# Modulation rows in four buffers, weights of the feed-forward tiles split two tiles ahead, and two mixer units in other banks, in a three-block float32 network on one core

## What is computed

```python
for layer in range(2):                          # blocks 1 and 2
    shift, scale, gate = split(c @ mod_w[layer, 0] + mod_b[layer, 0], 3)
    h = rms_norm(x, ...) * (1 + scale) + shift
    x = x + gate * rms_norm(mixer(h), ...)
    shift, scale, gate = split(c @ mod_w[layer, 1] + mod_b[layer, 1], 3)
    h = rms_norm(x, ...) * (1 + scale) + shift
    x = x + gate * rms_norm((silu(g) * u) @ w_out, ...)   # g, u = split(h @ w_in), width 2816
# block 3: modulation from silu(c_2) @ w_ada, its own mixer, then
z = conv3(h @ w_up) + b_conv;  a, b = split(z);  x = x + gt2 * ((silu(a) * b) @ w_down)
out = rms_norm(x, g_final)
```

## Time and profile before

| | us |
|---|---|
| three runs | 1174.82 median, 1167.96 to 1181.9 |
| the profiled execution | 1180.2 |
| its span in the profile | 1178.4 |
| TensorE matmul busy in the span | 1056.1 (90%) |
| VectorE busy | 791.8 (67%) |
| ScalarE busy | 552.5 (47%) |
| read from HBM | 225 MB, 192 GB/s over the span |

### The profile page before, as it was taken

The page is one execution under the profiler, slowest core; times in us unless marked ns, Lnnn a source line. Parts: engine busy times, 40 slices in busy tenths (PEclk is TensorE's granted clock), DMA queues, the critical chain, the costliest instruction groups (busy, mean ns, idle before and its releaser), DMA issues.

```text
span 1178.4 us, 21390 instructions
## 1 busy us (share of the span) xinstructions
PE 1056.1 (90%) x8164; PEld 1002.2 (85%) x8164; DVE 791.8 (67%) x1288; ACT 552.5 (47%) x1116; POOL 4.6 (0%) x14
## 2 busy tenths in 40 slices
PE   6988989988889979899988988988879879999996
PEld 5987778988889979799988887988857879999996
DVE  4649865766677656774766776765674757777775
ACT  2446755433333354454533333445441356666663
POOL 0100000000000000000000000000000000000000
PEclk9999989999999999999998999999875989999998
DMA  9966672667666637405376767664530354455530
GB/s 367 319 222 220 236 251 76 246 249 267 241 242 265 236 123 236 158 1 197 110 248 228 256 233 262 255 230 152 168 125 1 104 201 155 166 169 173 174 127 36
DMA packets 62405, 227.54 MB, mean 193 GB/s; under 512 B 7010, under 2 KB 7266, under 8 KB 61956
## 3 DMA queue, kind: packets, MB, share of 16 engines
q1 hardware_dynamic: 61556, 224.02, 53.6%
q0 software_dynamic: 640, 2.10, 0.7%
q10 hardware_dynamic: 144, 0.52, 0.1%
HBM read 225.04 MB, written 1.57 MB: 192 GB/s over the span
## 4 chain that ended last, share of the span: by engine, by line
PE 27%; DVE 24%; DMA 21%; issue 12%; ACT 12%; SPq 3%; DVEq 1%; ACTq 0%
DMA modbuf<-in_mod_w 12%; DMA modbuf<-in_w_ada 8%; DVE wL L1182 7%; ACT wH L766 5%; PE bank L1821 5%; PE bank L1822 4%; PE bank L1823 4%; DVE acc L589 2%; PE bank L1835 2%; PE bank L1836 2%; DVE proj L1383 2%; SPq L610 1%; DVE acc L1383 1%; PE bank L2428 1%; ACT pr L905 1%
## 5 line engine op out<-in xcount | busy, mean ns | idle before, releaser
L1821 PE MATMUL bank<-hH,wH 128*128 128x258 f32 (+1 forms) x1544 | 447.4, 290 | 15.0 <-DVE hL L1247 7.7
L1822 PE MATMUL bank<-hL,wH 128*128 128x258 f32 (+1 forms) x1544 | 440.0, 285 | 0.0
L1823 PE MATMUL bank<-hH,wL 128*128 128x258 f32 (+1 forms) x1544 | 438.1, 284 | 0.0
L1182 DVE TENSOR_TENSOR wL<-raw,wH 128x1024 fp32r<-128x1024 f32 x270 | 321.6, 1221 | 80.8 <-ACT wH L766 80.6
L1821 PEld LDWEIGHTS bank<-hH,wH 128*128 128x128 f32 x1544 | 294.7, 191 | 23.8 <-issue 14.8
L1822 PEld LDWEIGHTS bank<-hL,wH 128*128 128x128 f32 x1544 | 295.5, 191 | 0.5
L1823 PEld LDWEIGHTS bank<-hH,wL 128*128 128x128 f32 x1544 | 295.7, 191 | 0.0
L766 ACT ACTIVATE wH<-raw 128x1024 fp32r<-128x1024 f32 x270 | 271.1, 1045 | 35.9 <-DMA raw<-in_weights 18.6
L1821 PE MATMUL bank<-aH,wH 128*128 128x256 f32 x592 | 179.7, 304 | 58.9 <-DVE aL L1439 53.5
L1821 PEld LDWEIGHTS bank<-aH,wH 128*128 128x128 f32 x592 | 119.5, 202 | 69.6 <-DVE aL L1439 46.2
L1822 PE MATMUL bank<-aL,wH 128*128 128x256 f32 x592 | 173.7, 293 | 0.0
(11 more groups left out here) (313 smaller groups left out, 1188.3 us busy)
## 6 DMA issues: line engine op xcount, KB each, us to landing
raw<-in_weights SPq DMA_DIRECT2D x270, 512.0 KB, 4.5
modbuf<-in_mod_w SPq DMA_DIRECT2D x83, 512.0 KB, 5.0
modbuf<-in_w_ada SPq DMA_DIRECT2D x48, 512.0 KB, 5.0
strips<-bias_table POOLq DMA_DIRECT2D x8, 256.0 KB, 6.4
otok<-in_cmp_w SPq DMA_DIRECT2D x4, 512.0 KB, 8.6
raw<-in_mod_w SPq DMA_DIRECT2D x2, 512.0 KB, 4.8
otok<-in_mod_w SPq DMA_DIRECT2D x2, 512.0 KB, 10.5
sn<-in_mod_w SPq DMA_DIRECT2D x2, 512.0 KB, 11.9
```

The lines of the kernel that those rows point to most:

```text
L1182: V.tensor_tensor(wL[:, slot, :], raw[:, slot, :], wH[:, slot, :].bitcast(F32), ALU.subtract).then_inc(lo_ready[c], 1)
L1821: mm(out, lhs_h, rhs_h, start=start, stop=False, skip_group_check=True)
L1822: mm(out, lhs_h, rhs_l, start=False, stop=False, skip_group_check=True)
L1823: return mm(out, lhs_l, rhs_h, start=False, stop=stop, skip_group_check=True)
```

## The change

There are four row buffers for the jobs from f0 on (three in `modbuf`, one in `strips[:, 4:6]`), each with its own semaphore, and the load of job d waits until job d - 4 is done. In f0 and f1 the splits of a step are those of gate and up of tile t + 2 and of down(t+1): high and low of gate stand after silu and L1406, those of up after `aH` and `aL`, then comes the second job, then down. In f2 the low split of down(t) stands after the scaling and those of gate and up of tile t + 2 after the convolution and after L1436. In cd and sb units 2 and 3 go to banks 0 and 1, and only units from 4 on wait for a scaled one.

```diff
@@ -258,6 +258,7 @@
         lo_ready = [sem(f"lo_ready{i}") for i in range(3)]
         unit_used = [sem(f"unit_used{i}") for i in range(3)]
         mod_full = [sem(f"mod_full{i}") for i in range(2)]
+        job_full = [sem(f"job_full{i}") for i in range(4)]
         start_full = [sem(f"start_full{i}") for i in range(16)]
         mod_used = sem("mod_used")
         kc_zero = sem("kc_zero")
@@ -463,6 +464,8 @@
 
             if phase == "ab":
                 return bank[4 + AB_NUMBER[e] % 2]
+            if e in (2, 3):
+                return bank[e - 2]
             last = NPROJ[phase] - e
             return bank[4 + e % 2] if last > 2 else bank[4 - last]
 
@@ -527,6 +530,7 @@
             return a[:, at + j * P:at + (j + 1) * P]
 
         strips_flat = strips[:, :, :, :].rearrange("p a s j -> p (a s j)")
+        spare_job = strips[:, 4:6, :, :].rearrange("p a s j -> p (a s j)")
         third = [acc1[:, n * D:(n + 1) * D] for n in range(3)]
         start_slots = [raw[:, 4, :], raw[:, 5, :], otok[:, 0, :], sn[:, :, :].rearrange("p a b -> p (a b)"),
                        pr[:, :, :].rearrange("p a b -> p (a b)"), otok[:, 1, :], modbuf[:, 0, :], modbuf[:, 1, :],
@@ -537,14 +541,19 @@
 
         def job_value(d):
 
-            return 16 * ((d - JOBS_END["start"]) // 2 + 1)
+            if d < JOBS_END["ab"]:
+                return 16 * ((d - JOBS_END["start"]) // 2 + 1)
+            return 16 * ((d - JOBS_END["ab"]) // 4 + 1)
 
         def job_buffer(d):
 
             if d < JOBS_END["start"]:
                 q = ON_VECTOR[d]
                 return start_slots[q], start_full[q], 16
-            return modbuf[:, d % 2, :], mod_full[d % 2], job_value(d)
+            if d < JOBS_END["ab"]:
+                return modbuf[:, d % 2, :], mod_full[d % 2], job_value(d)
+            n = (d - JOBS_END["ab"]) % 4
+            return (modbuf[:, n, :] if n < 3 else spare_job), job_full[n], job_value(d)
         mod_src = [A["mod_w"][m] for m in range(4)] + [A["w_ada"][:, 0:MW], A["w_ada"][:, MW:2 * MW]]
 
         def cls(p):
@@ -612,7 +621,9 @@
             def load_job(d):
 
                 m, k, col, _, _ = JOBS[d]
-                if d >= JOBS_END["start"] + 2:
+                if d >= JOBS_END["ab"] + 4:
+                    sp.wait_ge(mod_used, d - 3)
+                elif JOBS_END["start"] + 2 <= d < JOBS_END["ab"] + 2:
                     sp.wait_ge(mod_used, d - 1)
                 dst, landed, _ = job_buffer(d)
                 sp.dma_start(dst, mod_src[m][k * P:(k + 1) * P, col:col + D]).then_inc(landed, 16)
@@ -694,9 +705,9 @@
                         for n in range(2):
 
                             d = d0 + 2 * t + n
-                            sp.wait_ge(mod_used, i * 4 + (d - 1))
+                            sp.wait_ge(mod_used, i * 4 + (d - 3))
                             src = mod_src[m + 1 + t % 2][bass.ds(i * P + P, P), n * D:(n + 1) * D]
-                            sp.dma_start(modbuf[:, d % 2, :], src).then_inc(mod_full[d % 2], 16)
+                            sp.dma_start(job_buffer(d)[0], src).then_inc(job_buffer(d)[1], 16)
 
                 assert Cursor.job == d0
                 step(0)
@@ -877,11 +888,7 @@
                     def at(n, per):
                         return n if i is None else i * per + n
 
-                    b = base + 3 * (t + 1)
-                    split = 1 <= t < FT - 1 or (t == FT - 1 and phase != "f2")
-                    if split:
-                        split_high(b, i)
-                        split_high(b + 1, i)
+                    nxt = base + 3 * t + 5
                     up_class, up_count = cls(base + 3 * t + 1)
                     act.wait_ge(unit_used[up_class], at(up_count, 2))
                     for n, bk in enumerate(gu_banks(phase, t)):
@@ -892,6 +899,7 @@
                         act.wait_ge(g_scaled, at(g0 + t + 1, 2))
                         nc.scalar.activation(sn[:, t % 2, 0:S], sn[:, t % 2, 0:S], ACT.Silu,
                                              bias=fcol[:, t % 2, 0:1]).then_inc(silu_ready, 1)
+                        split_high(nxt + 1, i)
                     else:
 
                         row = conv[:, t] if i is None else conv[:, bass.ds(i * 2 + t, 1)].rearrange("p o c -> p (o c)")
@@ -906,8 +914,9 @@
                                                         ACT.Identity, bias=row[:, 4 * n + 3:4 * n + 4],
                                                         scale=row[:, 4 * n + 1:4 * n + 2])
                         last.then_inc(zc_ready, 1)
-                        if split:
-                            split_high(b + 2, i)
+                        if nxt + 2 < N_UNITS:
+                            split_high(nxt + 1, i)
+                            split_high(nxt + 2, i)
                         act.wait_ge(conv_ready, at(t + 1, 2))
                         nc.scalar.activation(sn[:, t % 2, 0:S], pr[:, t % 2, 0:S], ACT.Silu).then_inc(silu_ready, 1)
                     act.wait_ge(af_ready, at(g0 + t + 1, 2))
@@ -916,11 +925,10 @@
                         down_class, down_count = cls(base + 3 * (t - 2) + 2)
                         act.wait_ge(unit_used[down_class], at(down_count, 2))
                     nc.scalar.activation(aH[:, t % 2, :], sn[:, t % 2, S:2 * S], ACT.Copy).then_inc(aH_ready, 1)
-                    if split and phase != "f2":
-                        if t == FT - 1:
-                            split_high(b + 3)
-                            split_high(b + 4)
-                        split_high(b + 2, i)
+                    if phase != "f2":
+                        split_high(nxt + 2, i)
+                    if 1 <= t and nxt < N_UNITS:
+                        split_high(nxt, i)
 
                 assert hi.at == base + RING
                 step(0)
@@ -1378,21 +1386,16 @@
                         cc = cvec[:, 0] if m + 1 + t % 2 < 4 else csil[:, :]
                         acc, at0 = JOBS[d][3:]
                         half = acc[:, at0:at0 + D]
-                        dve.wait_ge(mod_full[d % 2], i * 32 + job_value(d))
+                        dve.wait_ge(job_buffer(d)[1], i * 16 + job_value(d))
                         dve.wait_ge(mod_used, i * 4 + d)
-                        V.scalar_tensor_tensor(out=half, in0=modbuf[:, d % 2, :], scalar=cc[:, bass.ds(i + 1, 1)],
+                        V.scalar_tensor_tensor(out=half, in0=job_buffer(d)[0], scalar=cc[:, bass.ds(i + 1, 1)],
                                                in1=half, op0=ALU.mult, op1=ALU.add).then_inc(mod_used, 1)
 
                 def step(t, i=None):
                     def at(n, per):
                         return n if i is None else i * per + n
 
-                    b = base + 3 * (t + 1)
-                    split = 1 <= t < FT - 1 or (t == FT - 1 and phase != "f2")
-                    if split:
-                        split_low(b, i)
-                        if phase != "f2":
-                            split_low(b + 1, i)
+                    nxt = base + 3 * t + 5
                     dve.wait_ge(col_ready, at(g0 + t + 1, 2))
                     if t == 0:
                         dve.wait_ge(rstd_ready, NORMS.index(f"A{m}") + 1)
@@ -1406,12 +1409,12 @@
                         V.scalar_tensor_tensor(out=sn[:, t % 2, S:2 * S], in0=pr[:, t % 2, 0:S],
                                                scalar=fcol[:, t % 2, 1:2], in1=sn[:, t % 2, 0:S],
                                                op0=ALU.add, op1=ALU.mult).then_inc(af_ready, 1)
-                        job(1, t, i)
+                        split_low(nxt + 1, i)
                     else:
                         V.tensor_tensor(sq[:, t % 2, 0:S], gate_bank[:, 0:S], rstd[:, :], ALU.mult)
                         V.tensor_tensor(sq[:, t % 2, S:2 * S], up_bank[:, 0:S], rstd[:, :], ALU.mult).then_inc(gu_scaled, 1)
-                        if split:
-                            split_low(b + 1, i)
+                        if t >= 2:
+                            split_low(nxt - 3, i)
 
                         row = conv[:, t] if i is None else conv[:, bass.ds(i * 2 + t, 1)].rearrange("p o c -> p (o c)")
                         dve.wait_ge(zc_ready, at(t + 1, 2))
@@ -1429,20 +1432,22 @@
                                                          scalar=row[:, 4 * n + 2:4 * n + 3], in1=dst[:, 0:S - 1],
                                                          op0=ALU.mult, op1=ALU.add)
                         ins.then_inc(conv_ready, 1)
-                        if split:
-                            split_low(b + 2, i)
+                        if nxt + 2 < N_UNITS:
+                            split_low(nxt + 1, i)
                         dve.wait_ge(conv_ready, at(t + 1, 2))
                         dve.wait_ge(silu_ready, at(g0 + t + 1, 2))
                         V.tensor_tensor(sn[:, t % 2, S:2 * S], sn[:, t % 2, 0:S], pr[:, t % 2, S:2 * S],
                                         ALU.mult).then_inc(af_ready, 1)
```

(16 more changed lines are left out.)

## The result

The changed kernel takes 1235.05 us (median of 4 runs, 1232.1 to 1241.66), the kernel before 1177.68 us (4 runs). The ratio is 1.051, with a 95% interval of 1.042 to 1.059: slower by 5%, about 57 us. The profiled execution of the changed kernel took 1232.3 us with a span of 1230.5, 52 us over the span before.

The account below looks back on a forecast made before the run. Bound: in f0 and f1, a loop of low split, weight load, row DMA and VectorE's products. +74.5 (f0, f1) - 11 (f2) - 1 (mixers) = +62.5 us on the median 1174.8: 1237 us, range 1206 to 1262.

Parts of the forecast that it names:

- The loop, and that the buffers do nothing in it: f0 and f1: down's low split, SyncE's loads, row DMA, products, next low split form one loop; four buffers change nothing.
- Two splits on the path: f0 and f1: two splits of 1.14 us move behind the row, net +1.98 and +1.94 us a tile.
- The tail tiles, the start and the end: f0 and f1 outside the loop: one-row intervals +1.3 us each, 3.9 a stage; start +1.4, end +0.6.
- f2 at TensorE's pace: f2: period falls from 9.29 us to TensorE's 8.6 to 8.75; -11 us over 18 tiles, ends 0 and -14.
- The banks at about nothing: cd and sb: units 2 and 3 in banks 0 and 1; -1 us for both, ends 0 and -3.5.
- TensorE's pauses: f0 and f1: TensorE waits about 3.8 us a tile for `aL` instead of 1.8, 44 times, over 120 us in all.
- The clock rival: f0 and f1: pauses keep TensorE at 1.2 GHz, 17.3 us a tile, another +134, 1371 us; chance 0.05.
- the milder one: f0 and f1: rows land in 4.9 us, as transfers before are further apart; +31, 1206 us; chance 0.13.
- The faster one: f0 and f1: rows run ahead in four buffers, TensorE's 8.7 us a tile; 70 us shorter, 1105 us; chance 0.08.

Follow-up runs that it names:

- experiment 1: The changed kernel with two row buffers as before the change, all else kept; 1238.5 us, ratio 1.053 to the kernel before.
- experiment 4: The changed kernel with rows first: a step's row loads ahead of its three weight loads in SyncE's queue; 1110.1 us, ratio 0.944 to the kernel before.
- experiments 3 and 6: 3: changed kernel, f0/f1 splits in old places, 1166.6 us. 6: gate's split back, 1228.7; also second job, 1208.2; extra operation behind L1406, 1285.2, ahead of first product, 1236.3.
- experiment 7: The kernel before with only units 2 and 3 of cd and sb in banks 0 and 1; 1174.9 us against 1174.7, ratio 1.000.

## Why the prediction was right

It gave 1237 us, +62.5; measured are 1235 us and +57 (+50 to +70 by the interval of the ratio). The mechanism is the one that the experiments show. That the absolute times agree within 2 us is partly luck. The sum had f0 and f1 too large, +74.5 where 67 were measured in the profiled execution, and f2's gain too large as well, -11 where 7 were measured, so the two misses take from each other. And the sum started from a median before of 1174.8 us, where the one beside the result is 1177.7. The steps, one by one:

- **The loop, and that the buffers do nothing in it.** Shown. SyncE waits at the weight load before and after, experiment 1 has the loss with two buffers, and experiment 4, in which nothing but SyncE's order differs, removes the wait for the row altogether.
- **Two splits on the path, +2.28 a tile, less the second row's wait of 0.30 and 0.34.** Shown in kind by experiments 3 and 6. In size it was a little too much: +1.65 and +1.50 a tile were measured in place of +1.98 and +1.94. The term mis-sized is the time from the split of down to the first product, which I kept at 5.9 and 6.1 us. Its mean is 5.4 and 5.6 us in the changed kernel. But it did not fall by the change. In the kernel of experiment 7, with the old loop and 10.2 us a tile, it is 5.3 and 5.6 us. So I had taken it from an execution in which the rows land late: the first rows of f0's loop took 4.9 us in the median from issue to landing in the profiled execution before, and 4.2 us both in experiment 7 and in the changed kernel. Against experiment 7 a tile of the changed kernel is 1.90 and 1.84 us longer, close to what I forecast, though experiment 7 waits longer for its second rows, 0.65 and 0.49 us in the mean, than I had put. The profiled execution before lay 5.4 us over the median, and its f0 and f1 are 5.5 us longer than those of experiment 7; I took its stalls for those of every execution. In all f0 and f1 lost 67 us in the profiled execution (65.5 in the stages, 0.3 ahead and 1.2 behind) instead of 74.5, and 71 us in the stages against experiment 7.
- **The tail tiles, the start and the end.** Four of the six intervals between one-job tiles take 10.1 to 10.5 us as expected (9.26 + 1.3 = 10.6); in the other two a row lands late (12.84 us at tile 19 of f0, 11.60 us in f1). So the three of a stage cost +6.0 and +4.6 us where I had put +3.9. From the last L1406 to the next stage +0.6 us in both, as put.
- **f2 at TensorE's pace.** The period is 8.64 us in the mean of the last 19 intervals, and TensorE is busy all the time in the window shown. The gain is 7.0 us and not 11: the period of 9.29 that I took holds up to tile 16 only, the last intervals were at 8.8 us and less already, and the mean of the same 19 before was (1161.93 - 990.06)/19 = 9.05.
- **The banks at about nothing.** Measured 0, between the ends.
- **TensorE's pauses.** I had put 3.8 us a tile; the waits for `aL` are up to 4.0 us, but in all only this:

```profile
PE bank L1826 <- DVE aL L1444: 92.5, 40, 4.0
```

  The mean is 2.3 us, 92.5/40. The pause is shorter than I put since TensorE's own work takes longer: it is busy 128.74/13 = 9.9 us a tile in f0 and 10.1 in f1, where rows first has 8.65. The granted clock explains part of this. It is 0.94 and 0.90 in the two loops, where f1 had 0.96 before and rows first has 1.00. With the two levels of 2.4 and 1.2 GHz, a mean of 0.94 is 12% of 157.56 us at the lower one, of which half is lost: by this estimate 9.5 us, or 0.7 us a tile; in f1 it is 1.2. What makes up the rest of the 1.25 and 1.5 us is open. The clock rival was right about the sign of this and wrong about its weight: the loop of the rows, 12.1 us, is longer than TensorE's 9.9, so the time does not show it. One pause of f0's loop and the work behind it, in windows of PE, PEld, DVE, ACT, POOL, clock, DMA share and GB/s:

```profile
244.00:247.00 3.00, 0.42 (x4) 0.21 (x2) 2.46 (x3) 0.67 (x2) 0.00 (x0) 1.00 0.94 377
...
248.00:250.00 2.00, 2.00 (x10) 2.00 (x11) 2.00 (x2) 0.76 (x3) 0.00 (x0) 0.50 0.09 37
251.00:258.00 7.00, 7.00 (x59) 6.88 (x58) 2.49 (x5) 1.46 (x2) 0.00 (x0) 1.00 0.74 256
```

  The Trainium skill's page "TensorE: Matmul & The Clock Gate", section "HAM oscillation — how this bites in real kernels", describes a loop in which the clock falls again in every turn. Here it falls after some of the pauses only (between 220 and 280 us after two of four), and it costs nothing, for VectorE's loop sets the end.

Of the rivals, the milder one (rows that land in 4.9 us since the transfers are further apart) is not borne out: from split to first product it is 5.4 and 5.6 us, and no more than in the old loop of experiment 7. The faster one (1105 us) would have been right about the pace of f0 and f1 if the rows had run ahead: rows first gives 1110 us. Only its premise, that buffers are enough for it, was wrong.

## What to carry to other kernels

A deeper buffer is only worth something if the queue that fills it can get to the load in time: look at what stands ahead of the load in the issuing queue and what that waits for, before adding buffers. Here two buffers and a load moved up three places gave 5%, and four buffers without the move gave at most half a per cent.

In a loop that waits for a transfer, work on the waiting engine is free ahead of the wait, up to the wait's length, and costs its whole length behind it, as long as it doesn't fill another wait. Here one operation of 1.14 us in every tile cost 1.3 us in all ahead of it and 50 us behind it. So moving work off the start of a step is moving it out of its cover. Costs in such a loop don't add: taking one of two splits out gave 0.1 us, since a wait for another engine stood under it.

## What was not expected of the hardware

The time from issue to landing of the same row in the same place of the same queue differs between executions of one loop: the first rows of a tile in f0 took 4.9 us in the median in the profiled execution before, and 4.2 us in that of experiment 7, whose f0 has the same code. In the changed kernel, with its longer tiles, they took 4.2 us as well, so nothing here shows that the distance between the bursts makes the difference. In f1 the medians are 4.9, 4.6 and 4.8 us. The rows that go into the fourth buffer are all the second of their tile, issued some 0.6 us later, and their median is 6.1 us in the changed kernel. I have no experiment on what makes the rows of one execution later than those of another. A loop whose end hangs on such a row should be read from more than one profiled execution.

Four buffers alone made the kernel before faster by 0.5% (0.2 to 0.7), and no trace shows where. And the mixers, whose code was the same in most kernels, differ by 5 us in cd and 6 us in sb between single executions, so a gain of that size in a mixer can't be read from one profile.
